# A two-layer hybrid decoder trunk: TensorE multiplies a zero tile around its first column sums

## The reference, cut to what matters

```python
c_act = jax.nn.silu(c)
for layer in range(DEPTH):
    mod = c_act @ ada_w[layer] + ada_b[layer]
    sh_m, sc_m, g_m, sh_f, sc_f, g_f = [t[:, None, :] for t in jnp.split(mod, 6, axis=-1)]
    hm = x * (1.0 + sc_m) + sh_m
    ...  # mixer: hm @ w_in, then linear attention and mLSTM (layer 0) or attention (layer 1)
    x = layer_norm(RES_ALPHA * x + (1.0 + g_m) * y, ln_g[layer, 0], ln_b[layer, 0])
    hf = x * (1.0 + sc_f) + sh_f
    yf = swiglu(hf, ffn_w1[layer], ffn_w3[layer], ffn_w2[layer])
    x = layer_norm(RES_ALPHA * x + (1.0 + g_f) * yf, ln_g[layer, 1], ln_b[layer, 1])
```

## Time and profile before

| | us |
|---|---|
| runs | 1322.76, 1324.76, 1326.59 |
| median | 1324.76 |
| the profiled execution's own time | 1325.87 |
| its span (first to last instruction) | 1324.1 |
| mean granted TensorE clock | 0.996 |

### The profile page before, as it was taken

One profiled execution on the slowest core, in us unless ns is written; L12 is line 12 of the kernel. 1 busy time (PEld: TensorE's weight loads), 2 busy tenths in 40 slices (PEclk: granted clock), 3 DMA queues, 4 the chain that ended last, 5 costly groups with the idle time before them and its releaser, 6 DMA issues.

```text
span 1324.1 us, 17011 instructions
## 1 busy us (share of the span) xinstructions
PE 1278.8 (97%) x6438; PEld 1060.0 (80%) x6438; DVE 602.7 (46%) x936; ACT 476.9 (36%) x679; POOL 505.9 (38%) x209
## 2 busy tenths in 40 slices
PE   7999999999999999999999999989999999999996
PEld 6778878788888888888787777978888888878884
DVE  5489847868544443500658333367761111110005
ACT  3443344543332323212332565544442222322222
POOL 0243422323553434444335233311354444444444
PEclk9999999999999999999999999999999999999998
DMA  9982636622464646743236622230132232334312
GB/s 329 192 148 76 220 130 125 210 80 92 168 248 148 232 159 231 212 126 96 64 120 224 198 74 75 71 104 34 57 104 95 96 101 100 95 97 139 99 50 64
DMA packets 95331, 174.95 MB, mean 132 GB/s; under 512 B 15991, under 2 KB 63879, under 8 KB 95148
## 3 DMA queue, kind: packets, MB, share of 16 engines
q1 hardware_dynamic: 92136, 170.76, 42.5%
q10 hardware_dynamic: 3140, 3.43, 1.0%
HBM read 170.69 MB, written 4.52 MB: 132 GB/s over the span
## 4 chain that ended last, share of the span: by engine, by line
PE 79%; issue 10%; POOL 4%; DVE 4%; DMA 2%; ACT 1%; SPq 0%; POOLq 0%; DVEq 0%; ACTq 0%
PE ps L1157 15%; PE ps L1159 14%; PE ps L1158 14%; PE ps L1189 5%; PE ps L1191 5%; PE ps L1190 5%; POOL w_lo L714 3%; PE ps L1330 2%; PE ps L1332 2%; PE ps L1331 2%; PE ps L1296 1%; DMA ada_raw<-astream 1%; PE ps L1298 1%; PE ps L1297 1%; PE ps L1695 1%
## 5 line engine op out<-in xcount | busy, mean ns | idle before, releaser
L714 POOL TENSOR_TENSOR w_lo<-raw,w_hi 128x1024 fp32r<-128x1024 f32 x192 | 473.9, 2472 | 776.3 <-ACT w_hi L768 776.0
L1157 PE MATMUL ps<-h_lo,w_hi 128*128 128x512 f32 (+2 forms) x1064 | 397.8, 374 | 7.5 <-POOL w_lo L714 5.0
L1159 PE MATMUL ps<-h_hi,w_lo 128*128 128x512 f32 (+2 forms) x1064 | 393.9, 370 | 0.0
L1158 PE MATMUL ps<-h_hi,w_hi 128*128 128x512 f32 (+2 forms) x1064 | 393.8, 370 | 0.0
L768 ACT ACTIVATE w_hi<-raw 128x1024 fp32r<-128x1024 f32 x198 | 208.2, 1057 | 468.8 <-DMA raw<-wstream 172.9
L1157 PEld LDWEIGHTS ps<-h_lo,w_hi 128*128 128x128 f32 (+1 forms) x1064 | 200.3, 188 | 45.4 <-issue 8.0
L1159 PEld LDWEIGHTS ps<-h_hi,w_lo 128*128 128x128 f32 (+1 forms) x1064 | 200.3, 188 | 34.8
L1158 PEld LDWEIGHTS ps<-h_hi,w_hi 128*128 128x128 f32 (+1 forms) x1064 | 200.4, 188 | 33.2
L2360 DVE TENSOR_TENSOR tmp<-tmp,ps 128x512 f32<-128x512 f32 x44 | 30.2, 688 | 248.3 <-PE ps L1159 248.3
L1189 PE MATMUL ps<-w_hi,hid_lo 128*128 128x512 f32 x336 | 131.0, 390 | 1.7 <-issue 1.7
L1191 PE MATMUL ps<-w_lo,hid_hi 128*128 128x512 f32 x336 | 130.7, 389 | 0.0
(11 more groups left out here) (293 smaller groups left out, 1549.4 us busy)
## 6 DMA issues: line engine op xcount, KB each, us to landing
raw<-wstream SPq DMA_DIRECT2D x205, 512.0 KB, 4.3
ada_raw<-astream SPq DMA_DIRECT2D x80, 512.0 KB, 4.4
ada_first<-astream SPq DMA_DIRECT2D x16, 256.0 KB, 6.9
ada_first<-astream SPq DMA_DIRECT2D x8, 512.0 KB, 10.3
ln_rows<-row_scratch SPq DMA_DIRECT2D x3, 1024.0 KB, 6.4
skew_scratch<-f_scratch ACTq DMA_DIRECT2D x1, 2304.0 KB
xa<-xT SPq DMA_DIRECT2D x4, 512.0 KB, 9.2
out<-xa SPq DMA_DIRECT2D x3, 512.0 KB, 3.5
```

Of the source, the lines that this page charges most:

```text
L714: nc.gpsimd.tensor_tensor(w_lo[:, slot, :], raw[:, slot % RAW, :], w_hi[:, slot, :].bitcast(F32), ALU.subtract).then_inc(sem("w_lo_ready"), 1)
L1157: pe.matmul(o, w_h, x_l, start=start, stop=False)
L1158: pe.matmul(o, w_h, x_h, start=False, stop=False)
L1159: return pe.matmul(o, w_l, x_h, start=False, stop=stop)
```

## The change

A function `idle_turns(n)` on TensorE issues n matmuls of a tile with itself: the first 128 columns of the last chunk of `h_lo` as weights, its 512 columns as moving operand, into PSUM bank 3, each with start and stop set. Nothing reads the result; bank 3 is next written by `first_va(0)`, which starts a sum of its own there. DVE zeroes that chunk of `h_lo` ahead of its two small memsets, and a new semaphore `zeros` tells TensorE. `idle_turns` is called with 9 ahead of `first_cols(0)`, with 1 behind each of the four rows in it, and with 5 behind it.

```diff
             for k in FIRST_ON_PE[p]:
                 first_row(p, k, o, k == FIRST_ON_PE[p][0], False)
+                if p == 0:
+                    idle_turns(1)
             pe.wait_ge(sem("first_step"), first_steps(p + 1))
...
+        def idle_turns(n):
+
+            for _ in range(n):
+                pe.matmul(ps[:, 3, :], h_lo[:, KC - 1, 0:P], h_lo[:, KC - 1, :], start=True, stop=True, skip_group_check=True)
+
         assert pair("va") == 0 and pair("va+") == 2
+        pe.wait_ge(sem("zeros"), 1)
+        idle_turns(9)
         first_cols(0)
+        idle_turns(5)
...
+        V.memset(h_lo[:, KC - 1, :].bitcast(F32), 0.0).then_inc(sem("zeros"), 1)
         V.memset(ones[:], 1.0)
```

## The result

| | before | after |
|---|---|---|
| median, us | 1324.84 (22 runs) | 1328.35 (22 runs) |
| lowest to highest | 1322.76 to 1330.66 | 1324.72 to 1331.47 |
| ratio, with its 95% interval | | 1.0024 [1.0015, 1.0033] |
| the profiled execution's own time | 1325.87 | 1331.47 |
| its span | 1324.1 | 1329.7 |

The kernel after is slower by about 3.2 us. That lies inside the 0.3% which the forecast called the same, but the interval excludes no change, and the median is 0.35 us above the top of the range (1328.0). The profiled execution of after is one of its long ones, 3.1 us above its median, so its trace shows more loss than a typical execution has; a second profile of the same kernel, 1325.09 us, is read beside it further down.

What follows compares the result with a forecast made beforehand. DVE's chain was taken to set the pace up to 24.61 us, TensorE from 24.66 on; 1.4 us gained at the first products ends in a wait, so sum 0: 1325.9 profiled, 1324.8 on the median, range 1322.4 to 1328.0.

Steps and rivals of the forecast that it cites:

- The sum: Whole kernel: all parts net 0, so profiled 1325.87 us stays 1325.9, or 1324.8 put on the median.
- The cover of the memset and of the nine turns: Kernel start: memset hidden by over 2 us of cover; nine turns end about when the first row starts, cost 0 to 0.1.
- At 17.38 the clock should be up.: First large products: turns raise the clock before them, pitch 0.23 us at once; TensorE gains 1.4 us there.
- The gain of 1.4 us ends there.: Ahead of the second fold: TensorE waits for ada_acc until 24.61 regardless; wait grows from 0.70 to 2.1 us.
- C: Rival at the first rows: clock stays low, turns behind rows delay the fold, +0.2 to +1.05 us; chance 0.20.
- B: Rival at the second fold: longer wait lets the clock fall; fold +0.8, products +1.4, together +2.2 us, 1327.0; chance 0.17.
- No cost: The forecast case for the whole kernel: no net change, 1324.8 us (1323.5 to 1326 with code position and spread); chance 0.50.
- A delay of TensorE ahead of 25.58 is carried on.: From 24.66 us on the path is TensorE's; the stretch to ACT and POOL at 49.11 does not absorb a delay.
- Code position: Code behind the 18 added matmuls moves; a 1.2 us "issue" wait may come or go, -1.2 to +1.2, taken as 0.

Runs made afterwards that it cites:

- e2: Kernel before plus only the memset and the nine turns ahead of the first rows: 1325.07 us, ratio 0.9999.
- e3: Kernel before plus only the memset and one turn behind each of the four rows: 1330.65 us, ratio 1.0024.
- e10: Kernel after with DVE's copy of kc1 moved ahead of the last two steps of ada_acc near 711 us: 1332.99 us, ratio 1.0048.
- e4: Kernel before plus only the memset and the five turns in the pause behind the first fold: 1330.97 us, ratio 1.0040.
- e7: Kernel after with DVE's copy of kc1 moved one step of ada_acc earlier: 1325.26 us, ratio 1.0021.
- e16: Kernel after without the turns behind the rows and with three turns added ahead of the second fold: 1327.68 us, ratio 1.0004.
- e1: Kernel before once more, no edit: 1324.59 us, ratio 0.9995.
- e12: Kernel after once more, no further edit: 1328.73 us, ratio 1.0029.
- e15: Kernel after with the copy of the second bank of kc1 given from DVE to ACT: 1326.33 us, ratio 1.0008.
- e18: Kernel after with nine products of 256 columns in the wait at 657 us: 1327.54 us, ratio 1.0032.
- e6: Kernel before with DVE's copy of kc1 moved one step of ada_acc earlier: 1323.84 us, ratio 1.0002.
- e9: Kernel before with DVE's copy of kc1 moved ahead of the last two steps of ada_acc: 1330.87 us, ratio 1.0032.
- e14: Kernel before with the copy of the second bank of kc1 given from DVE to ACT: 1324.39 us, ratio 0.9991.
- e17: Kernel before with nine products of 256 columns in the wait at 657 us: 1325.45 us, ratio 1.0007.
- e19: Kernel before with both the second kc1 copy on ACT and nine products at 657 us: 1323.80 us, ratio 0.9996.
- e5: Kernel before, no turns, with one memset of 128x1024 on DVE ahead of its read of the first columns: 1326.14 us, ratio 1.0009.
- e13: Kernel before, no turns, with two memsets of 128x1024 on DVE ahead of the first columns' reading: 1326.95 us, ratio 1.0008.

## Why the prediction was wrong

Two steps failed. The sum put the turns behind the rows and the longer wait ahead of the second fold at nothing, and 16 of the 19 executions of after up to 1329 us stand some 2 or 3.4 us above the three that lose nothing. And the sum ended with the opening: a TensorE wait 700 us later grows from 1.4 to 4.0 us in after's profile, and executions above 1329 us went from 16% to 44%.

**The cover of the memset and of the nine turns.** Right. The memset took 0.48 us, the turns ran from 1.46 to 5.4, and e2 costs nothing.

**"At 17.38 the clock should be up."** Wrong, and without cost. In none of the profiles with turns was it up at the first product: where nine turns had raised it near 6 us it had fallen near 9, and it came back between 18.7 and 22.2. The argument had been that 3.9 us of dense work are enough for a rise, which is so in eight of the nine profiles that begin with nine turns, but by the mean clock not in 8 of the 34 executions of after (0.994 or 0.995), nor perhaps in three long ones at 0.993. What it left out is that the rows and the waits behind them let the clock go again before the products start. The Trainium skill (TensorE: Matmul & The Clock Gate, section Why this matters for your kernels) advises to leave no long idle gaps between bursts; here it went at 9.38 us without an idle gap, in rows of one-column matmuls with one turn each.

**"The gain of 1.4 us ends there."** Right in the main, and luckily so in part: it was read from an execution in which the fold waited 0.70 us, and in five of the seven profiles of that opening it does not wait at all and comes 0.22 to 0.63 us after `ada_acc`. There a higher clock gives that much back. The wait was forecast at 2.1 us and is 0.45 to 1.13 with five turns in the pause, since only part of the gain arose.

**C, the turns behind the rows delay the fold.** Right in mechanism and size (+0.95 in e3, up to 1.05 forecast). As the argument about the nine turns said, it needs rows at the lower level; of the profiles that have the nine turns and those behind the rows, one (e10) shows that. The mean clock says that a quarter to a third of after's executions were in that state, so the ground for taking nothing, that 3.9 us of dense turns raise the clock, was too weak.

**B, the clock falls again at the second fold.** Right in mechanism; the price was +2.2, of which 0.8 for a fold at the lower level. In after the fold at 24.18 still ran at the upper level (1.05 us) and only eight products fell, so B cost 1.6. It appears in five of the nine profiles that have the five turns in the pause (after, e4, e7, e10, e16), and in none of the eleven that lack them. The reason given, the longer wait, fits (it fell behind the four longest), but a wait that only one-column matmuls interrupt is not the condition: in e16 the fall came with turns in it. The point of a rise differs between executions of one opening (20.5 us in before's profile, 22.2 in e1), and a fall is there in the first profile of after and not in the second.

**The choice among the cases.** This was the first failure. No cost was given 0.50 on the ground that the traces showed a rise after 3.0 us of dense matmuls, B and C 0.37 together. In the six profiles of the full opening (after, e7, e10, e12, e15, e18) the shift behind it is +1.14, +1.01, +2.65, -0.64, -1.02 and -0.91 us: B in three, one of them with C. Openings without turns scatter from -0.33 to +0.01 (e1, e6, e9, e14, e17, e19). B and C together, +2.65, had no case of their own, and 8 of the 19 short executions of after stand where they would put them.

**"A delay of TensorE ahead of 25.58 is carried on."** Right for a plain delay (e5, e13), but the sum ended there, and this was the second failure, by means about as large as the first. By means, after is 2.9 us above before (1328.8 and 1325.9, outlier left out, 34 and 163 executions). The executions up to 1329 us have medians of 1327.1 and 1325.0. Above 1329 lie 15 of 34 (44%) against 26 of 163 (16%), at 1330.7 and 1330.0. By this split 1.4 us of the difference (28% more of them, some 5 us each) are long executions that became more frequent, and the other 1.5 is the first failure: not a shift of all executions, but the sets of the table above, of which the lowest stands where before's short ones do. The split hangs on the bound: some at 1329.1 may be of the opening alone. What a long execution consists of is shown for after and e3: TensorE waits 4.0 us at 714 us and the clock falls behind. With the copy out of the way, with and without the turns, long executions are about equally frequent (7 and 6 of 24) and the medians 1.4 to 1.9 us apart; that is what is left for the opening. That the turns lengthen executions by way of that wait is therefore argued from two traces and these counts, not shown for each long execution. In before with and without the edit long executions are about as frequent (6 of 24 and 26 of 163), so there are others with a place that no profile caught.

**What stays open.** Why the changed openings meet the long form at 714 us more often. It is not a late start (2 of 23 with a plain delay, 7 of 11 in e3 with a like one), and the fall at 661 us alone does not do it (e1). The last DVE step is long when POOL's subtraction starts first (below); of the thirteen profiles with the copy in its old place that is so for after and e3, and in the other eleven the step takes 1.28 or 1.29 us. Which of them is first is a matter of a tenth of a microsecond 700 us into the kernel; what sets it differently behind four turns than behind a memset is not known. Nor is it clear what the executions of e16 at 0.993 to 0.995 lose: they take 1328.0 to 1329.3 us, as the third set of after does, and that kernel has no turns behind the rows, so C cannot be their cause. This also leaves C's part in the third set open. Code position, which the prediction put at -1.2 to +1.2, was not tried by itself. The row that it was priced from is no such wait: in the earlier trace rows TensorE waits for the tile `id_far` of DVE, ready at 735.16, and starts at 735.26. It is 1.2 us long in after too.

## What to carry to other kernels

Turns that warm the clock pay only if the work right behind them is dense and TensorE is what the next stretch waits for. Here short rows and waits let the clock go again, and a DVE block set the end of the stretch, or came within 0.6 us of it; what was left were mostly the ways to lose. Ask of each added turn what it can delay, and of each wait that it lengthens whether the clock survives it. Look also at the later places where TensorE already waits a microsecond or more for another engine: there 2.5 us more of waiting cost 2.3 again behind it, at the lower clock. And compare the spread and the share of long executions, not two profiles: two profiled executions of after differ by 6.4 us, twice the effect. The mean granted clock of each execution tells whether the profiled one is typical.

## What the runs showed of the hardware that was not expected

Two engines at once on SBUF, and the first one wins where the starts are far enough apart to tell. A step of `ada_acc` on DVE (two inputs from SBUF) and a `w_lo` on POOL (also two) slow each other down. Timeline of DVE and POOL in after at 712 us:

```profile
712.41 2.37 POOL L714 TENSOR_TENSOR w_lo<-raw,w_hi 128x1024 fp32r<-128x1024 f32 x1 [1.65 <-ACT w_hi L768]
712.48 3.39 DVE L1910 SCALAR_TENSOR_TENSOR ada_acc<-ada_raw,c_act,ada_acc 128x1024 f32<-128x1024 f32 x1 [0.63 <-DMA ada_raw<-astream]
```

and in before:

```profile
711.30 1.28 DVE L1900 SCALAR_TENSOR_TENSOR ada_acc<-ada_raw,c_act,ada_acc 128x1024 f32<-128x1024 f32 x1 [0.66 <-DMA ada_raw<-astream]
711.67 3.13 POOL L714 TENSOR_TENSOR w_lo<-raw,w_hi 128x1024 fp32r<-128x1024 f32 x1 [2.11 <-ACT w_hi L768]
```

POOL starts 0.07 us ahead: POOL takes 2.37 us and DVE 3.39. DVE starts 0.37 us ahead: DVE takes 1.28 us and POOL 3.13. The Trainium skill (GPSIMD Engine Reference, section Specifications) names such contention for DVE instructions with two SBUF inputs. The traces agree, and in them the loser is longer by nearly all that is left of the winner's instruction: 2.11 us where POOL had 2.30 left, and 0.76 where DVE had 0.91. Where the two start practically together the outcome differs between executions. Before and e6 at 225 us, in that order:

```profile
225.72 3.48 DVE L1900 SCALAR_TENSOR_TENSOR ada_acc<-ada_raw,c_act,ada_acc 128x1024 f32<-128x1024 f32 x1
225.77 2.36 POOL L714 TENSOR_TENSOR w_lo<-raw,w_hi 128x1024 fp32r<-128x1024 f32 x1 [5.10 <-ACT w_hi L768]
```

```profile
225.12 1.28 DVE L1900 SCALAR_TENSOR_TENSOR ada_acc<-ada_raw,c_act,ada_acc 128x1024 f32<-128x1024 f32 x1
225.17 3.49 POOL L714 TENSOR_TENSOR w_lo<-raw,w_hi 128x1024 fp32r<-128x1024 f32 x1 [5.10 <-ACT w_hi L768]
```

The starts are 0.05 us apart in both, DVE's first, and DVE loses in the first and wins in the second. At this place it wins in four of the twenty profiles (e2, e4, e6, e18), with the same 0.05 us between the starts in all, and in these four TensorE is 1.4 us further forward behind 235 us. POOL's times in a profile are rough, but all twenty show one of these two pairs of lengths, within 0.01 us.
